# Products of 640 tokens cut at 512 and 128 columns instead of 320 and 320

## What is computed

```
x = x + 1/2 * SwiGLU_1(RMSNorm(x))          # 1024 -> 2 x 2816 -> 1024
u = RMSNorm(x); P = u @ w_in                # 1024 -> 9248 columns
branch A: conv (width 4) -> RG-LRU scan, times GeLU(gate), @ w_br_lru
branch B: conv -> SiLU -> chunked SSD scan, SiLU(z) gate, grouped RMSNorm, @ w_br_ssd
x = x + (sigmoid(gA) * A + sigmoid(gB) * B) @ w_out
x = x + 1/2 * SwiGLU_2(RMSNorm(x))
y = RMSNorm(x)                              # and the new states of both branches
```

## Time and profile before

| | us |
|---|---|
| median of 3 runs | 1846.12 |
| lowest and highest | 1845.39, 1846.13 |
| profiled execution | 1845.91 |
| its span, first to last instruction | 1844.0 |
| TensorE products on the fly | 1828.7 (99%) |
| VectorE busy | 1100.9 (60%) |
| ScalarE busy | 660.7 (36%) |
| GpSimd busy | 130.1 (7%) |

### The profile page before, as it was taken

The page is one execution under the profiler, slowest core; times in us unless marked ns, Lnnn a source line. Parts: engine busy times, 40 slices in busy tenths (PEclk is TensorE's granted clock), DMA queues, the critical chain, the costliest instruction groups (busy, mean ns, idle before and its releaser), DMA issues.

```text
span 1844.0 us, 31135 instructions
## 1 busy us (share of the span) xinstructions
PE 1828.7 (99%) x12565; PEld 1779.7 (97%) x12565; DVE 1100.9 (60%) x1354; ACT 660.7 (36%) x878; POOL 130.1 (7%) x258
## 2 busy tenths in 40 slices
PE   8999999999999999999999999999999999999998
PEld 8999999999999999989989989999999999999998
DVE  6443443345787875787787887877754433442444
ACT  5221332123477752344244235233342212221224
POOL 4000000000012210111101101100200000000000
PEclk9999999999999999999999999999999999999999
DMA  5222222222422253363454335336622222222222
GB/s 150 79 69 77 72 80 69 80 68 71 138 64 79 65 149 105 112 177 88 121 149 121 107 110 168 99 108 221 201 68 81 68 80 69 80 71 78 74 63 92
DMA packets 273102, 185.09 MB, mean 100 GB/s; under 512 B 7340, under 2 KB 260468, under 8 KB 272768
## 3 DMA queue, kind: packets, MB, share of 16 engines
q1 hardware_dynamic: 239984, 129.52, 24.5%
q0 software_dynamic: 10240, 35.86, 6.3%
q10 hardware_dynamic: 22800, 18.62, 3.1%
HBM read 161.43 MB, written 22.53 MB: 100 GB/s over the span
## 4 chain that ended last, share of the span: by engine, by line
PE 94%; DVE 3%; ACT 1%; DMA 1%; issue 1%; ACTq 0%; DVEq 0%
PE pu L660 86%; PE pn L893 1%; PE pn L786 1%; PE pn L916 1%; PE pn L935 1%; PE pn L910 1%; PE pu L968 1%; PE pn L882 0%; DVE w_lo L1521 0%; DMA gbuf<-gate_spill 0%; PE pn L947 0%; DVE squares L1515 0%; PE pn L677 0%; DVE x_lo L1515 0%; ACT w_hi L1033 0%
## 5 line engine op out<-in xcount | busy, mean ns | idle before, releaser
L1521 DVE TENSOR_TENSOR w_lo<-w_raw,w_hi 128x1024 fp32r<-128x1024 f32 x240 | 293.9, 1225 | 469.1 <-ACT w_hi L1033 467.8
L660 PE MATMUL pu<-act_hi,w_hi 128*128 128x320 f32 x1940 | 452.7, 314 | 1.5 <-DVE gbuf L1515 0.9
L660 PE MATMUL pu<-act_lo,w_hi 128*128 128x320 f32 x1940 | 442.9, 309 | 0.1
L660 PE MATMUL pu<-act_hi,w_lo 128*128 128x320 f32 x1940 | 442.4, 309 | 0.0
L1033 ACT ACTIVATE w_hi<-w_raw 128x1024 fp32r<-128x1024 f32 x240 | 253.7, 1057 | 520.8 <-PE pu L660 514.5
L660 PEld LDWEIGHTS pu<-act_hi,w_hi 128*128 128x128 f32 x1940 | 323.9, 188 | 16.5 <-issue 14.3
L660 PE MATMUL pu<-x_hi,w_hi 128*128 128x320 f32 x1440 | 328.9, 310 | 1.0 <-DVE w_lo L1521 0.5
L660 PE MATMUL pu<-x_lo,w_hi 128*128 128x320 f32 x1440 | 328.0, 309 | 0.0
L660 PE MATMUL pu<-x_hi,w_lo 128*128 128x320 f32 x1440 | 328.0, 309 | 0.0
L660 PEld LDWEIGHTS pu<-act_lo,w_hi 128*128 128x128 f32 x1940 | 324.8, 188 | 1.5 <-DVE act_lo L1566 0.7
L660 PEld LDWEIGHTS pu<-act_hi,w_lo 128*128 128x128 f32 x1940 | 325.1, 188 | 0.0
(11 more groups left out here) (339 smaller groups left out, 1876.8 us busy)
## 6 DMA issues: line engine op xcount, KB each, us to landing
w_raw<-in_ffn_w_up_dram SPq DMA_DIRECT2D x87, 512.0 KB, 3.8
w_raw<-in_w_in_dram SPq DMA_DIRECT2D x73, 512.0 KB, 3.9
w_raw<-in_ffn_w_down_dram SPq DMA_DIRECT2D x32, 512.0 KB, 3.6
da_rep<-e_spill POOLq DMA_DIRECT2D x20, 512.0 KB, 4.3
w_raw<-in_w_br_ssd_dram SPq DMA_DIRECT2D x16, 512.0 KB, 3.5
w_raw<-in_ffn_w_down_dram SPq DMA_DIRECT2D x16, 384.0 KB, 3.2
gate_spill<-gbuf ACTq DMA_DIRECT2D x17, 320.0 KB, 2.7
merged<-gate_spill POOLq DMA_DIRECT2D x8, 640.0 KB, 5.4
```

What stands on the lines that cost most here:

```text
L660: ins = pe.matmul(dst[:, h, :], w[:, side, c, :], a[:, k, h * HALF:(h + 1) * HALF], start=(at == 0), stop=(at == n - 1))
L1521: dve.tensor_tensor(w_lo[:, side, :, :], w_raw[:, side, :, :], w_hi[:, side, :, :].bitcast(F32), ALU.subtract).then_inc(s["w_lo_done"], 1)
```

## The change

Each pair of 320 + 320 columns is issued as 512 + 128 columns. The two banks of a buffer are taken as one run of 1024 values: the first matmul fills the first bank, the second the first 128 values of the next. `out_banks` gives those two pieces to TensorE. The readers get the same 640 values in order, still seen as two halves of 320 (`out`); the second half now begins at value 320 of the first bank and runs over the border. `last_unit` and its readers keep the old cut under the name `out_split`.

```diff
+BANK = 512
...
         def out(o):
 
+            return pu[o % 2][:, :, :].rearrange("p b n -> p (b n)")[:, 0:TOK].rearrange("p (h c) -> p h c", h=2)
+
+        def out_banks(o):
+
+            flat = pu[o % 2][:, :, :].rearrange("p b n -> p (b n)")
+            return [(flat[:, cut], cut) for cut in (slice(0, BANK), slice(BANK, TOK))]
+
+        def out_split(o):
+
             return pu[o % 2][:, :, 0:HALF]
...
-                        for h in range(2):
-                            ins = pe.matmul(dst[:, h, :], w[:, side, c, :], a[:, k, h * HALF:(h + 1) * HALF],
+                        for bank, cut in dst:
+                            ins = pe.matmul(bank, w[:, side, c, :], a[:, k, cut],
                                             start=(at == 0), stop=(at == n - 1))
...
-                products(out(ob), ub % 2, [(t, t) for t in range(nk)], hi, lo, ready, amid)
+                products(out_banks(ob), ub % 2, [(t, t) for t in range(nk)], hi, lo, ready, amid)
...
-                            ins = pe.matmul(out(o)[:, h, :], w[:, u % 2, k, :], a[:, k, h * HALF:(h + 1) * HALF],
+                            ins = pe.matmul(out_split(o)[:, h, :], w[:, u % 2, k, :], a[:, k, h * HALF:(h + 1) * HALF],
...
-                pair = pu[o % 2][:, :, 0:HALF].rearrange("p h (b c) -> p h b c", c=DEC_L)
+                pair = out(o).rearrange("p h (b c) -> p h b c", c=DEC_L)
```

More of the change, by code:

```diff
@@ L733, in first_unit @@
                 open_out(O_FFN1)
-                dst = out(O_FFN1)
+                dst = out_banks(O_FFN1)
                 for k in range(KT):
@@ L740, in first_unit @@
                             pe.wait_ge(s[name], XH_FFN1 + k + 1)
-                        for h in range(2):
-                            ins = pe.matmul(dst[:, h, :], w[:, 0, k, :], a[:, k, h * HALF:(h + 1) * HALF],
+                        for bank, cut in dst:
+                            ins = pe.matmul(bank, w[:, 0, k, :], a[:, k, cut],
                                             start=(k == 0 and a is x_hi and w is w_hi), stop=(k == KT - 1 and a is x_lo))
@@ L850, in branch_unit @@
                     open_out(o + m)
-                    products(out(o + m), u % 2, [(k, 2 * k + m) for k in range(PAIRS)], yn_hi, yn_lo,
+                    products(out_banks(o + m), u % 2, [(k, 2 * k + m) for k in range(PAIRS)], yn_hi, yn_lo,
                              ready=("yn_hi_done", "yn_lo_done", g * PAIRS, 0) if r == 0 and m == 0 else None)
@@ L1174, in to_ext @@
                 act.activation(ext[:, half + 1:LAST + 1, 0:HIST], pair[:, 1, 0:LAST - half, DEC_L - HIST:DEC_L], ACT.Copy).then_inc(s["ext_in"], 1)
-                act.activation(halves(dst), pu[o % 2][:, :, 0:HALF], ACT.Identity, scale=v(w), bias=v(bias)).then_inc(s["ext_in"], 1)
+                act.activation(halves(dst), out(o), ACT.Identity, scale=v(w), bias=v(bias)).then_inc(s["ext_in"], 1)
             def lru_front(j, first=False):
@@ L1626, in ffn @@
                                 dve.wait_ge(s["fin_half"], 1)
-                                stt(r, out(O_FIN - 1)[:, h, :], 0.25, r, ALU.mult, ALU.add).then_inc(s["fin_r"], 1)
+                                stt(r, out_split(O_FIN - 1)[:, h, :], 0.25, r, ALU.mult, ALU.add).then_inc(s["fin_r"], 1)
                             else:
@@ L1630, in ffn @@
                                 dve.wait_ge(s["out_ready"], O_FIN)
-                                stt(r, out(O_FIN - 1)[:, h, :], 0.25, r, ALU.mult, ALU.add).then_inc(s["out_free"], 1)
+                                stt(r, out_split(O_FIN - 1)[:, h, :], 0.25, r, ALU.mult, ALU.add).then_inc(s["out_free"], 1)
                             dve.wait_ge(s["fin_sq"], h + 1)
```

## The result

| | us | ratio to before |
|---|---|---|
| before, median of the runs beside it | 1845.82 | |
| with the change, median of 4 (2098.85 to 2100.0) | 2098.94 | 1.1372 (95% interval 1.1359 to 1.1386) |
| predicted | 2096, range 2020 to 2190 | |

The change makes the kernel 253 us slower, 13.7%. The prediction was 3 us low.

The account below looks back on a forecast made before the run. TensorE's stream of loads and products was taken as the bound. From 1845.9 us profiled, 5670 pairs at +44.4 ns (226.7 + 111 against 293.3) add 252 and swallowed waits take off 2: 2096 us, range 2020 to 2190.

Parts of the forecast that it names:

- The pace of TensorE is the time: Whole kernel: TensorE's stream of loads and products sets the end, L660 86% of the chain, 146.7 ns a product.
- The narrow step is the load's: 128-column products of L660: the next weights' load, 111 ns, sets the step, against 53 ns of streaming; chance 0.85.
- The lower bound of 108: Low end for the 128-column product's step, 108 ns; with 216 for the wide one, +31 ns a pair, +174 us.
- The wide step: 512-column product of L660: 226.7 ns taken, extra fixed at 13.3 per product; 234.7 if it grows with the columns.
- The pair: Each of 5670 pairs of 512 + 128 columns: 337.7 ns against 293.3, +44.4 ns, together +252 us.
- Waits swallowed, 2 us: TensorE's pauses at L660, 2.4 us in all: the slower stream swallows part, 2 us taken off.
- No change: Rival at the 5670 short products: the wide product's load is hidden or quicker than 0.11 us, about 1846 us; chance 0.05.
- The quicker load: Part of the no-change rival: loads before transposes (L882) have records 48 ns shorter, giving 63 ns instead of 111.
- The isolated gap of N / 2.4 + 2.5 ns: Skill rule weighed for L660's pairs: 320 + 320 costs as much as 512 + 128, 271.6 ns, so no change.
- Pace of f32 for short products: Rival at the 128-column products: 222 ns each as in f32, pair 449, +881 us, 2725 us; chance 0.05.
- Faster by the new cut: Rival at the pairs: the extra 13.3 ns vanishes and the load is hidden, pair 272 ns, -121 us, 1725 us; chance 0.02.
- The sign to look for: L660 in the timeline: wide product starts 111 ns after the short one, the short one 227 after the wide one.

## Why the prediction was right

- *The pace of TensorE is the time* (86% of the chain). Right: the loss is the pairs' times 5670, and the other engines' durations changed by 1% at most in their large groups.
- *The narrow step is the load's.* Right in mechanism, shown by the dose: 60 ns with 64 weight columns, 82 with 96, 108 with 128. In size it is 108 instead of 111. The 111 was read where short products follow each other; behind a wide one it is 108. What makes the 3 ns is open. The lower bound of 108 in the forecast stood on none of its rows, and the step came out there.
- *The wide step, 226.7 with a fixed extra or 234.7 with a proportional one.* Measured 232: I chose the worse of the two. The extra grows with the columns. Median steps of products that don't wait for weights: 60 at 128 columns, 117 at 256, 147 at 320, 177 at 384, 232 at 512, or 7, 10, 13, 17 and 19 ns beyond columns / 2.4 (448 columns, with 18 and 25, stands apart). The reason I gave, that something happens once per load or per product, does not fit: such a cost would be the same at all widths. The two runs with half loads show besides that the extra doesn't go with the load's length. What it is remains open.
- *The pair.* 340.0 against 337.7: two errors, +5 and -3, that partly cancel. 5670 x 46.7 = 265 us, 13 more than the 252 forecast.
- *Waits swallowed, 2 us.* Too small. Between the profiled executions the spans differ by 254.1, not 265. Summed over the distances of the ends of successive products, the pauses within the runs of units were 5.3 us before (0.7 of it in the first unit) and are 0.3 now: 5.0. I had counted only the 2.4 us that the profile lists as idle, and the drain of the product before a pause covers part of it in the records; that this is the whole difference was not tested. A further part is the 99 places where another kind of work follows a unit: the last narrow product's load isn't that of a wide product there, and a unit between two such places takes 8.12 us, not 24 x 0.340 = 8.16. By the trace 16 of the 99 keep a step of 108 ns all the same, and 51 have one near 60; the other 32 are followed by loads for a part of the array, and theirs can't be read. That is (99 - 16) x 0.047 = 3.9 us at most, 51 x 0.047 = 2.4 at least. The run with the narrow product first, which loses it, is 3.5 us slower than the change in the profiled executions. Some 1 to 3 us are not accounted for. The error of the pair and that of the waits are opposite too: terms that were off by 13 and 9 gave a sum 4 us under the profiled execution (2100.0) and 3 under the median. The mechanism was right; that the number came so close was luck.
- *Rivals.* No change (a load started early enough, or a quicker one): refuted by the time, and in the timeline no load of a unit starts before the product ahead. The quicker load was argued from the records of 140 ns before transposes, 48 less than 188, which gave 63 ns. For the transposes that was a good guess, as the changed kernel's trace shows at a unit's end:

```profile
817.52 0.20 PEld L892 LDWEIGHTS pn<-ident,xf 128*128 128x128 f32 x2
...
817.58 0.14 PEld L892 LDWEIGHTS pn<-ident,xf 128*128 128x128 f32 x1
```

  The unit's last narrow product has the first of these loads beside it, 128 weight columns too, and its step is 0.20 - 0.14 = 0.06. In all 47 places where a transpose's full load follows a unit, it is 57 to 63 ns. The units' own loads aren't of that kind: 108. The isolated gap of N / 2.4 + 2.5 ns that the Trainium skill gives ("TensorE: Matmul & The Clock Gate", "Back-to-back issue gap") does not hold for these products, neither for the sum nor for 512 columns alone: 215.8 by it, 232 here. Pace of f32 for short products: refuted, 60 ns with half a load. Faster by the new cut: refuted by the same cut in the new layout, 1847 us.
- *The sign to look for was partly wrong.* I wrote that the wide product would start 111 ns after the narrow one, and that a short product's step of 55 to 67 would make me wrong altogether. By the products' records the distance is 0.05 to 0.06 us, and yet the mechanism holds: these starts are taken before the weights are in. The earlier trace rows had shown it already, with loads 0.11 apart, where the product's record stands 0.03 behind the first load:

```profile
497.78 0.53 PE L660 MATMUL pu<-x_hi,w_hi 128*128 128x320 f32 x2 [0.42 <-DVE dt_raw L1717]
```

  The loads' starts are the ones to read.

## What to carry to other kernels

Where every product brings its own load of weights, a product's cost is, within a few ns, the longer of its stream and of the load beside it, which is the next product's, so a sum of columns is best cut in pieces none of which is shorter than a load: here the border lies between 192 and 256 columns for 128 x 128 weights. Fuller banks or a wider first piece bring nothing if the rest becomes too short. To find the load's time before a change, look for the shortest products behind full loads in the trace, and read the distance of the loads' starts.

## What the runs showed of the hardware

A load of the weights that stand in the array already costs a full load (second load of a pair with the narrow product first: 0.11 us). Among the units' products a load never starts before the product ahead. It is not so everywhere: the short products of L893, whose 64 weight columns go to one half of the partitions and the other in turn, have loads that start 0.10 us before the product ahead (140 of 320 in the kernel before). In the runs with half loads all such loads go to the same half, and none does. A load's time goes with the weight columns: 108 ns for 128, 82 for 96, at most 60 for 64 in the units' products. A transpose's load of 128 columns holds the narrow product ahead of it for no longer than 57 to 63 ns. The Trainium skill ("TensorE: Matmul & The Clock Gate", "LDWEIGHTS (loading the stationary operand)") gives columns / 1.2 ns, that is 107, 80 and 53; the units' loads agree at 128 and 96, and at 64 the stream of 60 hides the load; the transposes' loads do not agree, with at most 57 to 63 for 128. The Trainium skill ("TensorE: Matmul & The Clock Gate", "What happens when you issue a matmul") has it too that loading the next weights takes no read bandwidth from the running product; the 146.7 ns of a product of 320 columns, under half loads as under full ones, agree. Under full loads a narrow product of a unit right behind another takes 111 to 112 ns, behind a wide one mostly 108. Products of the same shape had two steps in some kernels, 205 and 210 to 213 ns for 448 columns, 231 and 238 for 512 with loads of 96; they go by the activations read, and no run here tells why. Reading 640 values over the border of two banks cost VectorE 815 ns against 814.
